# Expert results added into a table of sums by an accumulating indirect DMA, in place of rows stored and gathered at the end

## The chip, the cores and the metric

The kernel runs on one core of one Trainium2 chip, as one program with one launch. The metric is the device time of that core in microseconds (us); less is better. The engines of the core are TensorE (PE in the profile, with its weight loads as PEld), VectorE (DVE), ScalarE (ACT), GpSimd (POOL) and SyncE (SP). SP, ACT and POOL can issue DMA transfers, and 16 DMA engines carry them.

## The reference

The program computes two transformer blocks for 512 tokens of width 1024. The change touches only the last part of the second block, a layer of 32 routed experts followed by a layer norm. Cut to that part:

```python
logits = xt @ w_router + b_router                   # (512, 32)
top_vals, top_idx = lax.top_k(logits, 4)            # four experts for each token
gates = jax.nn.softmax(top_vals, axis=-1)
def expert_block(xb, e):
    gt = jnp.minimum(xb @ w_gate[e] + b_gate[e], 7.0)
    up = jnp.clip(xb @ w_up[e] + b_up[e], -7.0, 7.0)
    hid = gt * jax.nn.sigmoid(1.702 * gt) * (up + 1.0)
    return hid @ w_down[e] + b_down[e]
# for each token: the sum over its four experts of gate * expert_block(token, expert)
out = zeros.at[row_tok].add(y_rows * row_gate[:, None])
x = layer_norm_2(DEEPNORM_ALPHA_2 * h + out, ln2_g, ln2_b)
```

All numbers are float32. The matrices of one expert (gate, up and down) are 1024 x 1024 each, so 12 MB for one expert.

## The kernel before

The program is a list of stages, written by hand: every engine has its own instruction list in each stage, and semaphores join them. Nothing is scheduled by a planner. Between two stages all engines meet, and SP clears the semaphores of the stage that ended. Six earlier stages compute the first block and the attention of the second. One of them, `stage_ffn`, has no part in the experts, but its ACT list begins with transfers that write zeros to device memory. Then come the three stages that matter here.

`stage_route` scores the experts, picks four for each token, and packs the 2048 choices into **slots** of 64 rows (`CAP`), each slot with one expert. The number of slots is known only on the chip (`G.last_slot`); with these inputs there are 45. A loop over 16 columns of choices (`TK`) ends the stage: DVE makes a one-hot of the row in the slot (`colhot`) and a one-hot of the slot times twice the token number (`slothot`), and PE multiplies the two and accumulates. DVE turns the sum into `G.slot_tokens`, the list of rows to gather for each slot. It also computes `G.choice_row`, the place of each choice in the table of results.

`stage_experts` makes one **pass** per slot. A slot's 64 rows are held on 128 partitions, as two halves of 512 columns. In pass i, PE does the first half of the gate product of slot i, then transposes the hidden values of slot i-1 (`turn_h`) and the gathered rows of slot i+1 (`turn_x`), then the second half of gate(i), then down(i-1), then up(i). SP streams the matrices of the next expert into `expert_ring` (4 MB for each of the three matrices, in four parts) as soon as the last pass of the present expert has used a part. POOL gathers the rows of slot i+1 by an indirect DMA into `slot_x`; there is one such buffer, so the gather waits for the transpose of the slot before. DVE evicts down(i-1) from PSUM into `slot_y` (`result`), and ACT stores it with two plain transfers to `expert_rows` (`store`). There is one `slot_y` too: the next `result` waits for the stores.

`stage_final` reads the results back. POOL gathers 16 times 128 rows of 4 KB (four tiles of 128 tokens, four choices each) into eight buffers `choice_y`; DVE scales each by its gate and adds it into `ffn_sum`, adds ALPHA times `X`, and does the moments and the normalizing of the layer norm (class `Norm`); ACT takes the root; POOL multiplies by the gain and adds the shift (`gain_shift`); SP stores the tile.

Of the kernel before, what the change touches and what calls it, by code (L numbers as in the profile page):

```python
# [7 lines left out]
F32 = mybir.dt.float32  # L8
# [7 lines left out]
P = 128  # L16
# [1076 lines left out]
def stage_ffn(nc, A, G):  # L1093


    with ExitStack() as ctx:
# [15 lines left out]
        @block.sync  # L1112
        def _(sp):
            ln.load(sp)
            G.W.upto(sp, G.W.index[("q2",)] + RING)
            sp.wait_ge(G.y_zeroed, 16 * (-(-(MAX_SLOTS - EXPERTS) * CAP // P)))
# [427 lines left out]
def stage_route(nc, A, G):  # L1544
# [6 lines left out]
    with ExitStack() as ctx:  # L1551
# [20 lines left out]
        tok2 = sb("token_twice", [P, T])  # L1572
        upper = sb("upper_half", [P, 1])
# [12 lines left out]
        rowf = sb("choice_rowf", [P, TK])  # L1586
        colhot = sb("col_onehot", [P, 2, P])
        slothot = sb("slot_token", [P, 2, LIST])
        cmp_ = sb("slot_compare", [P, LIST, E])
        sef = sb("slot_expertf", [P, LIST])  # L1590
        names = "in lg_done iota_ok step exp_ok mem_ok cnt_done hot_ok hot_used list_done neg_ok".split()
# [9 lines left out]

        @block.gpsimd
# [12 lines left out]
        def _(pe):  # L1615
# [23 lines left out]
        def _(dve):  # L1639
# [4 lines left out]
            nc.vector.tensor_scalar(tok2[:], tok[:], 2.0, None, ALU.mult)  # L1644
# [3 lines left out]
            nc.vector.tensor_scalar(upper[:], tok[:, 0:1], float(CAP), None, ALU.is_ge)  # L1648
# [55 lines left out]
            step(nc.vector.tensor_reduce(sl[:], pick[:], AX_X, ALU.add))  # L1704
            step(nc.vector.tensor_tensor(sl[:], sl[:], over[:], ALU.add))
            for c in range(TK):
                if c >= 2:
                    dve.wait_ge(q["hot_used"], c - 1)
                nc.vector.tensor_scalar(colhot[:, c % 2, :], rank[:], col[:, c:c + 1], None, ALU.is_equal)
                nc.vector.tensor_scalar(slothot[:, c % 2, :], iota[:, 0:LIST], sl[:, c:c + 1],  # L1710
                                        tok2[:, c // TOP_K:c // TOP_K + 1], ALU.is_equal, ALU.mult).then_inc(q["hot_ok"], 1)
# [4 lines left out]
            step(nc.vector.tensor_scalar(G.slot_tokens[:], ps[:, 3, 0:LIST], upper[:, 0:1], None, ALU.add))  # L1716
# [33 lines left out]
def stage_experts(nc, A, G):  # L1750
# [5 lines left out]
    with ExitStack() as ctx:  # L1756
        def sb(name, shape, dt=F32):
# [7 lines left out]
        ids = sb("slot_ids", [P, 1], I32)  # L1765
        gt = sb("gate_act", [P, HALF])
# [7 lines left out]
                 "y_ok").split()  # L1774
# [36 lines left out]
        def _(pool):  # L1811
# [21 lines left out]
            pool.wait_ge(q["x_turned"], 1)  # L1833
            gather(1)
            last = loop(pool, body)

            pool.wait_ge(G.xg_in, last * 16 + 32)

            pool.wait_ge(G.y_out, last * 32 + 32)

        @block.scalar
        def _(act):
# [18 lines left out]
            def store(i):  # L1861
                act.wait_ge(q["y_ok"], i + 1)
                for h in range(2):
                    act.dma_start(G.y_dram[bass.ds(i * CAP, CAP), h * HALF:(h + 1) * HALF],
                                  y[h * CAP:(h + 1) * CAP, :]).then_inc(G.y_out, 16)

            def body(i, first):
# [5 lines left out]
                if not (isinstance(i, int) and i == 0):  # L1873
                    store(i - 1)
# [288 lines left out]
```

## Time and profile before

| | |
|---|---|
| Device time, median of 3 runs | 2791.09 us (2789.03 to 2792.38) |
| The profiled execution's own time | 2787.3 us |
| Its span in the profile | 2785.6 us |
| Granted TensorE clock, mean | 0.933 of full speed |
| Busy share of the span: PE, DVE, ACT, POOL | 89%, 22%, 11%, 10% |
| Bytes moved by DMA | 570.63 MB, mean 205 GB/s |
| Stage of the routing, from the span's start | 1407.2 to about 1456 us |
| Stage of the experts | about 1456 to 2723.3 us |
| Last stage | 2723.3 to 2785.6 us |

How to read it: the shares are means over stages with different limits. The profiled execution is one run; its time stands 3.8 us under the median of the three timed runs. A sum that is made against the profile is carried over to the median by the difference that it gives.

### The profile page before, as it was taken

To read this page: it belongs to the slowest core of one execution; us is meant where nothing else is said; L and a number is where in the kernel's file an instruction comes from. 1 tells how busy PE (TensorE), PEld (TensorE's weight loads), DVE (VectorE), ACT (ScalarE), POOL (GpSimd) and SP (SyncE) were. 2 spreads that over 40 slices of the span, in tenths; PEclk is the share of its full clock that TensorE was granted. 3 is DMA by queue.
4 is the path that set the end of the run, shared out by engine and by line. 5 is a ranking of instruction groups with operands and counts; after the bars stand their busy time and mean duration, and the time that the engine had idled before them with its cause. 6 is when DMAs were issued, how large, how long until landed. Compare 5 with 4: busy or idle time off the path is not lost. (4 is left out here: it accounts for less than half of the span.)

```text
span 2785.6 us, 25073 instructions
## 1 busy us (share of the span) xinstructions
PE 2474.5 (89%) x9812; PEld 1029.4 (37%) x9813; DVE 601.4 (22%) x1283; ACT 293.8 (11%) x598; POOL 277.8 (10%) x290
## 2 busy tenths in 40 slices
PE   4999999798999999895949889999999889998990
PEld 3445666343444444343443223333332223322320
DVE  1322566521000002223341101111111101110116
ACT  0111222300000000012001000100100000100000
POOL 0003111011101011111210000000000000000005
PEclk8999999899999999998959989999999989999995
DMA  7353222204312211300049998778768998879844
GB/s 290 118 202 89 76 84 91 83 0 187 126 61 91 91 60 46 137 31 0 23 195 357 419 421 312 275 264 339 302 218 339 421 418 314 333 297 421 318 179 168
DMA packets 191387, 570.63 MB, mean 205 GB/s; under 512 B 14751, under 2 KB 49692, under 8 KB 189276
## 3 DMA queue, kind: packets, MB, share of 16 engines
q1 hardware_dynamic: 172288, 526.05, 49.2%
q10 hardware_dynamic: 12764, 22.25, 2.3%
q0 software_dynamic: 6272, 21.50, 2.1%
q8 instruction: 39, 0.64, 0.1%
q14 instruction: 24, 0.20, 0.0%
HBM read 545.57 MB, written 24.18 MB: 205 GB/s over the span
## 5 line engine op out<-in xcount | busy, mean ns | idle before, releaser
L1907 PE MATMUL banks<-expert_ring,slot_xT_gate 128*64 128x512 f32 x1440 | 371.4, 663 | 67.7 <-DMA expert_ring<-in_w_gate_dram 67.0
L1907 PE MATMUL banks<-expert_ring,hiddenT 128*64 128x512 f32 x1440 | 320.6, 598 | 0.7 <-ACT hiddenT L1855 0.7
L1907 PE MATMUL banks<-expert_ring,slot_xT_up 128*64 128x512 f32 x1440 | 318.9, 595 | 0.0
L1160 PE MATMUL banks<-hT,weight_ring 128*128 128x512 f32 x512 | 223.8, 598 | 6.8 <-PEq L2080 4.6
L1178 PE MATMUL banks<-weight_ring,hidden_T 128*128 128x512 f32 x512 | 220.7, 593 | 1.5 <-PE banks L1160 1.1
L1907 PEld LDWEIGHTS banks<-expert_ring,slot_xT_gate 128*64 128x64 f32 x1440 | 108.9, 151 | 294.9 <-issue 278.5
L1907 PEld LDWEIGHTS banks<-expert_ring,hiddenT 128*64 128x64 f32 x1440 | 99.8, 137 | 217.8 <-issue 216.9
L1907 PEld LDWEIGHTS banks<-expert_ring,slot_xT_up 128*64 128x64 f32 x1440 | 99.4, 137 | 216.4 <-issue 216.4
L1160 PEld LDWEIGHTS banks<-hT,weight_ring 128*128 128x128 f32 x512 | 97.4, 192 | 132.7 <-issue 132.7
L1914 PE MATMUL banks<-bias_rows,ones 1*64 1x512 f32 x540 | 145.0, 613 | 0.0
L1178 PEld LDWEIGHTS banks<-weight_ring,hidden_T 128*128 128x128 f32 x512 | 97.0, 190 | 125.3 <-issue 125.3
L461 PE MATMUL banks<-hT,weight_ring 128*128 128x512 f32 x320 | 141.7, 603 | 0.0
L1952 DVE TENSOR_SCALAR gate_act<-banks 128x512 f32<-128x512 f32 x45 | 31.1, 692 | 469.8 <-PE banks L1914 469.8
L1820 POOL COPY slot_ids<-slot_tokens 128x1 int32 (+1 forms) x46 | 8.3, 181 | 1117.5 <-PE banks L1888 1117.4
L1050 PE MATMUL banks<-weight_ring,mixT 128*128 128x512 f32 x256 | 112.0, 600 | 5.0 <-DVE mixT L1073 5.0
L702 PE MATMUL banks<-hT,weight_ring 128*128 128x512 f32 x256 | 115.5, 606 | 0.0
L1960 DVE TENSOR_SCALAR up_act<-banks 128x512 f32<-128x512 f32 x45 | 31.1, 692 | 323.2 <-PE banks L1914 323.2
L1851 ACT COPY slot_xT_up<-banks 128x512 f32<-128x512 f32 x46 | 27.0, 586 | 651.7 <-PE banks L1914 651.7
L1972 DVE COPY slot_y<-banks 128x512 f32<-128x512 f32 x45 | 31.1, 692 | 276.8 <-PE banks L1914 276.8
L461 PEld LDWEIGHTS banks<-hT,weight_ring 128*128 128x128 f32 x320 | 61.4, 194 | 79.0 <-issue 79.0
L1050 PEld LDWEIGHTS banks<-weight_ring,mixT 128*128 128x128 f32 x256 | 49.0, 192 | 67.9 <-issue 58.7
L1203 DVE TENSOR_TENSOR ffn_out<-ffn_out,banks 128x512 f32<-128x512 f32 x24 | 16.5, 688 | 245.6 <-PE banks L1178 245.6
(349 smaller groups left out, 2067.1 us busy)
## 6 DMA issues: line engine op xcount, KB each, us to landing
expert_ring<-in_w_gate_dram SPq DMA_DIRECT2D x128, 1024.0 KB, 10.3
expert_ring<-in_w_up_dram SPq DMA_DIRECT2D x128, 1024.0 KB, 16.5
expert_ring<-in_w_down_dram SPq DMA_DIRECT2D x128, 1024.0 KB, 7.9
weight_ring<-in_w_ada_dram SPq DMA_DIRECT2D x12, 2048.0 KB, 11.4
weight_ring<-in_w_in_dram SPq DMA_DIRECT2D x8, 2048.0 KB, 13.6
weight_ring<-in_w_ff_in_dram SPq DMA_DIRECT2D x8, 2048.0 KB, 8.5
weight_ring<-in_w_ff_out_dram SPq DMA_DIRECT2D x8, 2048.0 KB, 7.9
weight_ring<-in_w_in_dram SPq DMA_DIRECT2D x24, 512.0 KB, 6.6
```

The costliest lines, as they stand in the source:

```text
L461: m = nc.tensor.matmul(ps[:, n % 4, :], w[:, k, b * P:(b + 1) * P], G.hT[:, k, :], start=(k == 0), stop=(k == KB - 1))
L702: x = nc.tensor.matmul(out, w[:, k, :], G.hT[:, k, :], start=(k == 0), stop=(k == KB - 1))
L1050: m = nc.tensor.matmul(ps[:, 2 * t + h, :], G.mixT[:, k, t * P:(t + 1) * P], w[:, k % 4, h * HALF:(h + 1) * HALF], start=(k == 0), stop=(k ...
L1160: m = nc.tensor.matmul(ps[:, n % 4, :], w[:, k, (b % 4) * P:(b % 4 + 1) * P], G.hT[:, k, :], start=(k == 0), stop=(k == KB - 1))
L1178: m = nc.tensor.matmul(ps[:, 4 + n % 4, :], aT[:, g % 2, k, t * P:(t + 1) * P], w[:, k % 4, h * HALF:(h + 1) * HALF], start=(k == 0), stop ...
L1203: nc.vector.tensor_tensor(y, y, ps[:, 4 + n % 4, :], ALU.add).then_inc(dn_read, 1)
L1851: nc.scalar.copy(flat(xTu), ps[:, B_X, :]).then_inc(q["xu_ok"], 1)
L1907: x = nc.tensor.matmul(ps[h * CAP:(h + 1) * CAP, bank, :], lhs[:, k % 4, (k // 4) * CAP:(k // 4 + 1) * CAP], X.ring[:, m, k, h * HALF:(h + ...
L1914: x = nc.tensor.matmul(ps[h * CAP:(h + 1) * CAP, bank, :], G.ones[0:1, 0:CAP], X.rows[0:1, m, h * HALF:(h + 1) * HALF], start=False, stop= ...
L1952: nc.vector.tensor_scalar(gt[:], ps[:, B_G, :], 7.0, None, ALU.min).then_inc(q["g_read"], 1)
L1960: nc.vector.tensor_scalar(up[:], ps[:, B_U, :], 7.0, -7.0, ALU.min, ALU.max).then_inc(q["u_read"], 1)
L1972: nc.vector.tensor_copy(y[:], ps[:, B_D, :]).then_inc(q["y_ok"], 1)
```

## The change

The results of the experts are no longer stored as rows and gathered at the end. A table `expert_sums` with one row for each token (1024 half rows, and 128 more as a place for the padding of the slots) is set to zero in `stage_ffn`. In the route stage POOL makes a second one-hot, of the slot times the gate, and the same matrix product then gives both the rows and the gates of every slot (`G.slot_gates`). In each pass DVE scales the evicted result by the slot's gates, and POOL adds the 128 half rows to the table by an indirect DMA with an addition. Each such addition is issued after the one before has landed. The last stage loads four tiles of sums with plain transfers. The core of the diff:

```diff
 # stage_ffn, ACT
-            for r in range(EXPERTS * CAP, MAX_SLOTS * CAP, P):
-                n = min(P, MAX_SLOTS * CAP - r)
-                act.dma_start(G.y_dram[r:r + n, :], zeros[0:n, :]).then_inc(G.y_zeroed, 16)
+            for t in range(T):
+                act.dma_start(sums[t * P:(t + 1) * P, :], zeros[:]).then_inc(G.y_zeroed, 16)
+            for table in (G.sum_dram, G.h_dram):
+                act.dma_start(table.rearrange("(r h) n -> r (h n)", h=2)[S:S + CAP, :], zeros[0:CAP, :])\
+                   .then_inc(G.y_zeroed, 16)
...
 # stage_route, POOL
+            pool.wait_ge(q["sl_ok"], 1)
+            for c in range(TK):
+                if c >= 2:
+                    pool.wait_ge(q["hot_used"], c - 1)
+                nc.gpsimd.tensor_scalar(slothot[:, c % 2, LIST:], iota[:, 0:LIST], over[:, c:c + 1],
+                                        gates[:, c:c + 1], ALU.is_equal, ALU.mult).then_inc(q["gate_hot_ok"], 1)
 # stage_route, PE
                 pe.wait_ge(q["hot_ok"], c + 1)
-                nc.tensor.matmul(ps[:, 3, 0:LIST], colhot[:, c % 2, :], slothot[:, c % 2, :], start=(c == 0),
+                pe.wait_ge(q["gate_hot_ok"], c + 1)
+                nc.tensor.matmul(ps[:, 3, 0:2 * LIST], colhot[:, c % 2, :], slothot[:, c % 2, :], start=(c == 0),
                                  stop=(c == TK - 1)).then_inc(q["hot_used"], 1)
 # stage_route, DVE
+            nc.vector.scalar_tensor_tensor(out=val[:].rearrange("p (t k) -> p t k", k=TOP_K),
...
+            nc.vector.tensor_copy(over[:], sl[:]).then_inc(q["sl_ok"], 1)
...
-            step(nc.vector.scalar_tensor_tensor(out=rowf[:], in0=sl[:], scalar=float(CAP), in1=col[:], op0=ALU.mult,
-                                                op1=ALU.add))
-            nc.vector.tensor_copy(G.choice_row[:], rowf[:])
             dve.wait_ge(q["hot_used"], TK)
+            nc.vector.tensor_copy(G.slot_gates[:], ps[:, 3, LIST:2 * LIST])
...
 # stage_experts, POOL
-            def body(i, first):
-                pool.wait_ge(q["x_turned"], i + 1)
-                gather(i + 1)
+            def scatter(i):
+                if not (isinstance(i, int) and i == 0):
+                    pool.wait_ge(G.y_out, i * 16)
+                    pool.wait_ge(q["y_ok"], i)
+                at = slice(i, i + 1) if isinstance(i, int) else bass.ds(i, 1)
+                nc.gpsimd.tensor_copy(share[:], G.slot_gates[:, at]).then_inc(q["share_ok"], 1)
+                nc.gpsimd.tensor_copy(out_ids[:], G.slot_tokens[:, at]).then_inc(q["out_ids_ok"], 1)
+                pool.wait_ge(q["out_ids_ok"], i + 1)
+                pool.wait_ge(q["y_ok"], i + 1)
+                nc.gpsimd.tensor_tensor(tick[:, 2:3], tick[:, 0:1], tick[:, 0:1], ALU.add).then_inc(q["result_held"], 1)
+                nc.gpsimd.indirect_dma_start(G.sum_dram[:, :], bass.IndirectOffsetOnAxis(out_ids[:, 0:1], 0), y[:], None,
+                                             compute_op=ALU.add).then_inc(G.y_out, 16)
...
+            with pool.Fori(2, last + 1) as i:
+                pool.wait_ge(q["x_turned"], i + 1)
+                gather(i + 1)
+                scatter(i - 1)
+            scatter(last)
 # stage_experts, ACT: store() and its two act.dma_start are gone
 # stage_experts, DVE
+                dve.wait_ge(q["share_ok"], i + 1)
                 if not first:
-                    dve.wait_ge(G.y_out, i * 32)
-                nc.vector.tensor_copy(y[:], ps[:, B_D, :]).then_inc(q["y_ok"], 1)
+                    dve.wait_ge(G.y_out, i * 16)
+                nc.vector.tensor_scalar(y[:], ps[:, B_D, :], share[:, 0:1], None, ALU.mult).then_inc(q["y_ok"], 1)
 # stage_final
+            for t in range(T):
+                sp.dma_start(sums[:, t, :], rows[t * P:(t + 1) * P, :]).then_inc(sum_in[t], 16)
...
-            for c in range(TK):
-                if c >= 8:
-                    pool.wait_ge(added, c - 7)
-                nc.gpsimd.indirect_dma_start(yk[:, c % 8, :], None, G.y_dram[:, :],
-                                             bass.IndirectOffsetOnAxis(G.choice_row[:, c:c + 1], 0))\
-                    .then_inc(in_[c % 8], 16)
...
+            ln.load(act)
...
+            for t in range(T):
+                dve.wait_ge(sum_in[t], 16)
+                nc.vector.scalar_tensor_tensor(out=G.X[:, t, :], in0=G.X[:, t, :], scalar=ALPHA, in1=sums[:, t, :],
+                                               op0=ALU.mult, op1=ALU.add).then_inc(ln.u_ok, 1)
+                ln.moments(dve, t)
+                ln.norm(dve, t)
```

The first place is the loop of POOL over the passes. Before, one turn of it is these rows (`slot_ids` is the list of rows for the gather, `tick` a dummy that keeps two instructions in order):

```order
L1820 COPY slot_ids<-slot_tokens 128x1
L1821 REGISTER_ALU
L1815 TENSOR_TENSOR tick<-tick 1x1
L1823 DMA slot_x<-h_halves,slot_ids 128x512
L1789 ISA
L1789 COMPARE_AND_BRANCH
```

And one turn of it in the changed kernel (`slot_gate` and `slot_out_ids` are the gates and the destination rows of the slot whose result is due):

```order
L1840 COPY slot_ids<-slot_tokens 128x1
L1841 REGISTER_ALU
L1835 TENSOR_TENSOR tick<-tick 1x1
L1843 DMA slot_x<-h_halves,slot_ids 128x512
L1848 ISA
L1851 ISA
L1851 COPY slot_gate<-slot_gates 128x1
L1852 REGISTER_ALU
L1852 COPY slot_out_ids<-slot_tokens 128x1
L1855 TENSOR_TENSOR tick<-tick 1x1
L1856 DMA expert_sums<-slot_y,slot_out_ids 1152x512
L1869 ISA
```

The gather now has a second indirect DMA behind it on the same engine, and the gather of the next turn stands behind that one's waits.

The second place is DVE in the last stage, one tile of four. Before:

```order
L2035 TENSOR_SCALAR ffn_sum<-choice_y,choice_gates 128x1024
L2032 SCALAR_TENSOR_TENSOR ffn_sum<-choice_y,choice_gates,ffn_sum 128x1024 x3
L2038 SCALAR_TENSOR_TENSOR X<-X,ffn_sum 128x1024
L961 BN_STATS ln2b_stats<-X 128x6
L962 BN_STATS ln2b_stats<-X 128x6
```

In the changed kernel, where `ffn_sum` holds the loaded sums:

```order
L2052 SCALAR_TENSOR_TENSOR X<-X,ffn_sum 128x1024
L961 BN_STATS ln2b_stats<-X 128x6
L962 BN_STATS ln2b_stats<-X 128x6
L963 BN_AGGR ln2b_mv<-ln2b_stats 128x2
L964 TENSOR_SCALAR ln2b_mv<-ln2b_mv 128x1
```

Four instructions of each tile are gone, and those of the layer norm follow one another directly.

## Rows read from the trace of the kernel before

**Rows 1.** Windows of the experts' stage: us, five engines' busy time, PE clock, DMA share, GB/s

```profile
1528.00:1685.90 157.90, 136.84 (x582) 43.18 (x580) 17.30 (x25) 11.92 (x20) 6.75 (x15) 0.90 1.03 420
1690.00:1860.00 170.00, 170.00 (x786) 53.84 (x784) 23.54 (x34) 16.70 (x28) 9.45 (x21) 1.00 0.74 274
```

**Rows 2.** Waits of PE from 1456 us on: total, times, longest

```profile
PE banks L1907 <- DMA expert_ring<-in_w_gate_dram: 67.0, 19, 4.9
```

**Rows 3.** Windows of the last stage, columns as in rows 1

```profile
2723.30:2735.70 12.40, 0.00 (x0) 0.00 (x0) 4.61 (x5) 1.28 (x1) 8.99 (x10) 0.50 0.91 338
2735.70:2777.70 42.00, 0.00 (x0) 0.00 (x0) 39.30 (x40) 0.81 (x4) 24.67 (x13) 0.50 0.43 162
2777.70:2785.60 7.90, 0.00 (x0) 0.00 (x0) 0.00 (x0) 0.00 (x0) 4.67 (x2) 0.50 0.17 66
```

**Rows 4.** Timeline of the last stage, DVE on the second and third tile

```profile
2744.82 1.23 DVE L2038 SCALAR_TENSOR_TENSOR X<-X,ffn_sum 128x1024 f32<-128x1024 f32 x1
2748.27 1.52 DVE L974 TENSOR_SCALAR X<-X,ln2b_mv 128x1024 f32<-128x1024 f32 x1
2752.64 3.17 DVE L2032 SCALAR_TENSOR_TENSOR ffn_sum<-choice_y,choice_gates,ffn_sum 128x1024 f32<-128x1024 f32 x1
```

**Rows 5.** The same on POOL, third tile

```profile
2764.85 2.78 POOL L982 TENSOR_TENSOR X<-X,ln2b_gb 128x1024 f32<-128x1024 f32 x1 [6.84 <-DVE X L974]
2767.71 3.20 POOL L984 TENSOR_TENSOR X<-X,ln2b_gb 128x1024 f32<-128x1024 f32 x1
```

**Rows 6.** Chain that ended last: start us, us, what; first tile's first and last

```profile
2735.70 1.23 DVE X L2038
...
2739.14 0.81 DVE X L974
```

**Rows 7.** DMA issues of the page: count, KB each, median us to landing

```profile
X<-in_x_dram SPq DMA_DIRECT2D x4, 512.0 KB, 5.6
out_dram<-X SPq DMA_DIRECT2D x4, 512.0 KB, 2.6
```

**Rows 8.** DMA queues of the page: packets, MB, share of 16 engines

```profile
q1 hardware_dynamic: 172288, 526.05, 49.2%
q10 hardware_dynamic: 12764, 22.25, 2.3%
```

**Rows 9.** Landing times of all gathers of slot_x, then of all stores

```profile
DMA to landing us min/median/max: 3.2/5.9/6.6
DMA to landing us min/median/max: 2.3/5.6/7.9
```

**Rows 10.** Timeline, one gather of POOL, and the last passes

```profile
2655.04 0.18 POOL L1820 COPY slot_ids<-slot_tokens 128x1 int32 x1 [28.96 <-PE banks L1888]
2655.86 0.99 POOL L1823 DMA_INDIRECT slot_x<-h_halves,slot_ids  x1 [0.37 <-issue]
2667.63 0.69 DVE L1972 COPY slot_y<-banks 128x512 f32<-128x512 f32 x1 [6.04 <-PE banks L1914]
2679.51 0.60 PE L1888 MATMUL banks<-ident,slot_x 128*128 128x128 f32 x4
2692.87 0.69 DVE L1972 COPY slot_y<-banks 128x512 f32<-128x512 f32 x1 [6.04 <-PE banks L1914]
2713.53 0.69 DVE L1972 COPY slot_y<-banks 128x512 f32<-128x512 f32 x1 [11.32 <-PE banks L1914]
2714.40 1.13 ACTq L1864 DMA_DIRECT2D expert_rows<-slot_y  x2
```

**Rows 11.** Groups of the route stage by shape: busy us, mean ns

```profile
L1635 PE MATMUL banks<-slot_token,col_onehot 128*128 128x64 f32 x32 | 8.9, 435 | 10.1 <-DVE slot_token L1710 10.1
```

**Rows 12.** Transposes of slot_x on PE: duration ns min/median/max

```profile
L1888 PE MATMUL banks<-ident,slot_x x184: 272/273/476, 1460.7 to 2679.8; 128*128 128x128 f32 x184
```

**Rows 13.** Timeline of the start of the ffn stage

```profile
679.18 29.90 PE L1160 MATMUL banks<-hT,weight_ring 128*128 128x512 f32 x64 [4.64 <-PEq L2080]
680.13 15.59 ACTq L1135 DMA_DIRECT2D expert_rows<-zeros  x16
```

More of the change, by code:

```diff
@@ L1600, in _ @@
             G.experts.prefetch(sp)
+        gates = G.gates[:].rearrange("p t k -> p (t k)")
         @block.gpsimd
@@ L1765, in stage_experts @@
         ids = sb("slot_ids", [P, 1], I32)
+        out_ids = sb("slot_out_ids", [P, 1], I32)
+        share = sb("slot_gate", [P, 1])
         gt = sb("gate_act", [P, HALF])
@@ L1832, in _ @@
             gather(0)
-            pool.wait_ge(q["x_turned"], 1)
-            gather(1)
-            last = loop(pool, body)
+            for i in (1, 2):
+                pool.wait_ge(q["x_turned"], i)
+                gather(i)
+            scatter(0)
+            last = pool.value_load(G.last_slot[0:1, 0:1], min_val=EXPERTS - 1, max_val=MAX_SLOTS - 1)
+            with pool.Fori(2, last + 1) as i:
[3 more added lines that the diff above has]
+            scatter(last)
             pool.wait_ge(G.xg_in, last * 16 + 32)
-            pool.wait_ge(G.y_out, last * 32 + 32)
+            pool.wait_ge(G.y_out, last * 16 + 16)
         @block.scalar
@@ L1859, in sigmoid @@
                 nc.scalar.activation(sg[:], gt[:], ACT.Sigmoid, scale=1.702).then_inc(q["sg_ok"], 1)
[L1861 to L1865, printed above, removed]
             def body(i, first):
@@ L1872, in body @@
                 sigmoid(i)
-                if not (isinstance(i, int) and i == 0):
-                    store(i - 1)
                 act.wait_ge(q["u_done"], i + 1)
@@ L1881, in _ @@
             h_turned(last)
-            store(last)
         @block.tensor
@@ L1993, in stage_final @@
         sem = G.sem
-        yk = sb("choice_y", [P, 8, D])
-        acc = sb("ffn_sum", [P, D])
-        in_ = G.choice_in
-        added, acc_step, out_done = sem("added"), sem("acc_step"), sem("out_done_all")
+        sums = sb("ffn_sum", [P, T, D])
+        sum_in = [sem(f"sum_in{t}") for t in range(T)]
+        out_done = sem("out_done_all")
         ln = Norm(nc, ctx, G, "ln2b", A["ln2_g_2"][0:1, :], A["ln2_b_2"][0:1, :])
+        rows = G.sum_dram.rearrange("(r h) n -> r (h n)", h=2)
         block = ctx.enter_context(nc.Block())
@@ L2026, in _ @@
         def _(dve):
-            for c in range(TK):
-                t, k = c // TOP_K, c % TOP_K
-                dve.wait_ge(in_[c % 8], 16 * (c // 8 + 1))
-                if k:
-                    dve.wait_ge(added, c)
-                    nc.vector.scalar_tensor_tensor(out=acc[:], in0=yk[:, c % 8, :], scalar=G.gates[:, t, k:k + 1],
-                                                   in1=acc[:], op0=ALU.mult, op1=ALU.add).then_inc(added, 1)
-                else:
-                    nc.vector.tensor_scalar(acc[:], yk[:, c % 8, :], G.gates[:, t, 0:1], None, ALU.mult).then_inc(added, 1)
-                if k == TOP_K - 1:
-                    dve.wait_ge(added, c + 1)
-                    nc.vector.scalar_tensor_tensor(out=G.X[:, t, :], in0=G.X[:, t, :], scalar=ALPHA, in1=acc[:],
-                                                   op0=ALU.mult, op1=ALU.add).then_inc(ln.u_ok, 1)
-                    ln.moments(dve, t)
-                    ln.norm(dve, t)
+            for t in range(T):
[4 more added lines that the diff above has]
+                ln.norm(dve, t)
 def make_shared(nc, ctx, A):
@@ L2064, in make_shared @@
     G.gate_bias_in, G.xg_in = sem("gate_bias_in"), sem("xg_in")
-    G.choice_in = [sem(f"choice_in{i}") for i in range(8)]
     return G
```

35 lines of the change are left out of this document (20 added, 15 removed).

## The prediction

> **What bounds the kernel now.** I read the windows of the experts' stage first, then the waits of PE, then the last stage. In the experts' stage the reader should see two kinds of passes. Where each pass brings a new expert, as in the 157.9 us from 1528.0 to 1685.9, which hold five passes (31.6 us each), the DMA engines are full: share 1.03 at 420 GB/s, and PE is busy for 136.84 us at a granted clock of 0.90 [rows 1]. Where experts have several slots, as from 1690 to 1860, PE is busy all the time at full clock and the DMA share is 0.74 [rows 1]; such a pass takes 25.24 us, the distance of two evictions of the result (2667.63 and 2692.87) [rows 10]. PE's wait for the gate matrix, 67.0 us in 19 waits [rows 2], counts the passes of the first kind: 19. So a microsecond more of DMA work per pass is paid 19 times in full and elsewhere not at all.
>
> The last stage is a chain of its own: 12.4 us until the first gathered rows are added, 42.0 us in which DVE is busy for 39.30 us, and 7.9 us of POOL and the last store, 62.3 us together [rows 3].
>
> **The last stage, removed and left.** The 16 gathers and 16 weighted additions go. What is left: four loads of 512 KB, then for each tile DVE's addition of ALPHA times X and the layer norm. The first tile lands after about 4.0 us: a lone 512 KB store takes 2.6 us and four loads in a row have a median of 5.6 us [rows 7]; the gain and the shift now come from another queue at the same time, so I take a value between them. The first tile's DVE work, uncovered by POOL, is 4.25 us, from the addition at 2735.70 to the end of the normalizing at 2739.14 + 0.81 [rows 6]. For tiles two to four, DVE's addition now starts exactly when POOL starts the gain of the tile before. An addition of this form beside POOL took 3.17 us, against 1.23 us without it [rows 4]; so 4.25 + 1.94 = 6.2 us per tile. POOL needs 2.78 + 3.20 = 6.0 us per tile beside DVE [rows 5], just under that. If the normalizing is slowed too (1.52 us once, against 0.81) [rows 4, 6], it is 6.9 us. The tail of 7.9 us stays [rows 3]. Sum: 4.0 + 4.25 + 3 x 6.2 + 7.9 = 34.75 us, in place of 62.3: **-27.5 us**. Bounds: 32 us (tile one at 3, nothing slowed twice) to 38 us (5.6 and 6.9), so -30 to -24.
>
> **The pass: DMA work.** The stores leave ACT's queue, and 256 KB per pass go by an accumulating DMA. A copy of 0.262 MB costs, at the rate of ACT's queue (22.25 MB in 2.3% of 2785.6 us on all 16 engines), 0.75 us of all 16 engines [rows 8]; at the rate of the weights' queue (526.05 MB in 49.2%) it is 0.68 us [rows 8]. The trace shows no accumulating transfer. It must bring in two streams, the result and the old sum, and write one. Lower bound of its extra price: 0, if the read of the old sum hides in the pipeline of reads and writes. Likeliest: the input side carries twice the bytes, so it costs one copy more, 0.7 us. Upper bound: each row waits for memory before the next goes. Nearly all of the shortest store's 2.3 us [rows 9] is fixed time, and each engine has 8 of the 128 rows, so up to 8 x 2.3 - 0.7 = 18 us per pass. That end is far, but nothing in the trace excludes it. I take 0.7, since an engine that is full at 1.03 with three kinds of transfers in flight shows that the queues overlap well [rows 1]: 19 x 0.7 = **+13.3 us**. The Trainium skill (DMA: Bandwidth & Descriptors, "SDMA does more than copy") calls the addition an inline unit that reduces two streams and gives no price for it; no run here has shown it yet. By the reading that inline means free, this term would be 0 and the total 13.3 us lower.
>
> **The pass: the order on POOL.** Before, the gather of slot i+2 left as soon as slot i+1 was transposed, a pass ahead. Now it stands behind the addition of result i-1, which waits for DVE's eviction. Take the pass at 2667.63 [rows 10]: the result is out at 2668.3, the dummy and the issue of the addition take about 0.5 + 1.0 us, the turn of the loop about 0.3, then copy of the list to start of the gather 2655.86 - 2655.04 = 0.8 us. The gather starts at about 2671. Landing takes 3.2 to 6.6 us [rows 9], so 2674.3 to 2677.7; the rows are wanted by the transpose at 2679.5. The slack is 1.8 us at worst. The addition's traffic is ahead of the gather on the same queue, which I price at up to a copy or two, 0.7 to 1.4 us. So it fits, barely, and costs 0. In the long passes there are 6 us more. Where the cover is gone, each lost microsecond stands on PE's path in up to 24 short passes. The other waits are long over: the gates of slot i are copied a pass ahead of `result`, and the addition before has landed some 15 us before the next eviction. DVE's scaled eviction is of the same form and shape as the copy. ACT loses two issues and waits for nothing else. For the last pass, the store issued at 2714.40 with its 1.13 us for two issues landed at about 2715.05 + 2.3 = 2717.3 [rows 9, 10]. The addition starts at about 2715.0 and lands after the shortest gather, 3.2 us [rows 9], plus an estimated 1.2 for the second read: 2719.4. **+2.1 us**, bounds 0.5 and 6.
>
> **The route stage.** The matrix product of each choice goes from 64 to 128 columns. At the same low clock one PE instruction takes 435 ns for 64 columns [rows 11] and 476 for 128 [rows 12]; two per choice, and one choice in two lies on the ring of DVE and PE, so 8 x 2 x 0.04 = 0.7 us. DVE adds two small operations and a copy on its path, 0.4 us by their size, and drops two that lay beside PE. POOL's one-hot has no row; from 2.78 us for 1024 columns of two inputs [rows 5], 64 columns are 0.17 us plus a start of about 0.2 (its copy of one column takes 0.18 [rows 10]); it runs beside DVE's two operations. Bounds 0 and 0.3 us for each of 8 rounds. Sum **+1.5 us**, 0.5 to 4. Five more semaphores to clear: 0.2 us.
>
> **The zeros.** Ten of 16 transfers go from the start of the ffn stage, where ACT spends 15.59 us issuing them [rows 13]. PE works through its 64 products from 679.18 on for 29.90 us in one piece [rows 13], which covers ACT's issues: 0. Without that cover the fewer issues would be a gain of some 9 us.
>
> **Sum.** Against the profiled execution's own 2787.3 us: -27.5 + 13.3 + 2.1 + 1.5 + 0.2 = -10.4, so 2776.9. That execution stands 3.8 us under the median, so in the medians it is 2791.1 - 10.4 = **2780.7 us**.
>
> **Rivals.**
> - *The second stream is free.* The price per pass is under 0.3 us; total -24 to -18 us, 2767 to 2773. For it: writes and reads are separate sides of a transfer. Against it: the DMA share of 1.03 leaves no gap for more reads [rows 1]. Chance 0.22.
> - *The accumulating transfer is slow* (the other side of zero). Place: the 19 full passes. It decides from 23.7 / 19 = 1.25 us more per pass on, where the gain is used up. At four times a copy, 2.1 us more, it costs 40 us, total +16: 2807. At the far end, 18 us per pass, it is +300 us. For it: additions in the transfer path work on elements, and nothing shows their rate. Chance 0.25, of which a fifth above 2820.
> - *The gather comes late.* Place: the transpose of `slot_x` in the short passes. It decides when the addition holds the queue for over 1.8 us. Each microsecond late in the half of 24 short passes with loads in flight is 12 us, so 2 us late gives -10.4 + 24 = +14: 2804. Against it: the shortest landing leaves 5 us. The Trainium skill (DMA: Bandwidth & Descriptors, "Two DMAs through the same engine are not ordered") says that only the completion semaphore orders transfers, and the diff waits for one per pass; by it the wait stands on POOL alone, as worked out above. Chance 0.08.
> - *The last stage gives little*, because the loads or DVE beside POOL take longer: -15 instead of -27.5, total +2: 2793. Chance 0.05.
> - My forecast, -17 to -3 us, 2774 to 2788: chance 0.40.
>
> **Numbers.** The measurement tells 0.2% (5.6 us) from no change. Faster by more: all of the first rival, most of the forecast (down to 0.9 us per pass) and a little else, 0.56. Within 0.2%: 0.17. Slower: 0.27. The range of eight in ten is 2765 to 2815; the forecast's own is 2774 to 2788.
>
> **What would show it.** The last stage 33 to 37 us long, with DVE's addition of tiles two to four near 3.2 us. The full passes near 32.3 us in place of 31.6, the short ones still 25.24, with no wait of PE for `slot_x`. Landing of the additions 4 to 9 us. The route stage 1 to 2 us longer. I am wrong if the full passes grow by over 1.3 us, or if short passes are longer than 25.3 us.

## The result and the profile after

The changed kernel takes 2800.0 us, the median of 10 runs (2797.61 to 2801.23), against 2791.09 us for the kernel before (10 runs, 2787.16 to 2795.17). The ratio is 1.0031 with an interval of 1.0021 to 1.0040: **slower by 0.3%**, 8.9 us, where 10.4 us less were forecast. The two profiled spans stand 12.7 us apart, 2785.6 and 2798.3 us. The granted clock is no cause: its mean is 0.933 before and 0.934 after.

A **full pass** is here one of the 19 in which PE waits for the gate matrix [rows 2], a short one any other. First the windows, the view of [rows 1] and [rows 3]: the same five full passes near the stage's start, then the last stage in three stretches. The columns are the busy times of PE, PEld, DVE, ACT and POOL with their counts, the clock, the DMA share and GB/s.

```profile
1534.99:1699.30 164.31, 136.89 (x582) 43.34 (x580) 17.59 (x25) 11.93 (x20) 17.54 (x35) 0.91 1.03 401
2760.85:2767.24 6.39, 0.00 (x0) 0.00 (x0) 0.00 (x1) 1.28 (x1) 0.00 (x0) 0.50 0.81 250
2767.24:2790.41 23.17, 0.00 (x0) 0.00 (x0) 21.52 (x28) 0.81 (x4) 16.70 (x6) 0.50 0.28 112
2790.41:2798.30 7.89, 0.00 (x0) 0.00 (x0) 0.00 (x0) 0.00 (x0) 4.68 (x2) 0.50 0.33 133
```

Five full passes take 164.31 us in place of 157.9. PE's busy time is the same to 0.1 us (136.89 and 136.84 us), and the DMA share is at 1.03 as before, but it carries 401 GB/s where it carried 420 [rows 1]. So the DMA engines are as full as they were and move less. The last stage takes 6.39 + 23.17 + 7.89 = 37.45 us in place of 62.3 [rows 3].

The waits of PE from 1450 us on (total, times, longest), in the view of [rows 2]:

```profile
PE banks L1934 <- DMA expert_ring<-in_w_gate_dram: 96.5, 19, 6.3
PE banks L1915 <- DMA slot_x<-h_halves,slot_ids: 6.6, 1, 6.6
PE banks L1648 <- POOL slot_token L1616: 2.1, 5, 0.4
```

The 19 waits for the gate matrix grew from 67.0 to 96.5 us, by 29.5. The wait for `slot_x` is the one of the very first pass, before which nothing has been loaded. The third row is in the route stage: PE waits there for POOL's one-hot, which didn't exist before.

The queues of the page, as [rows 8] (packets, MB, share of 16 engines), then two of its DMA issues (count, median us from issue to landing):

```profile
q1 hardware_dynamic: 172576, 527.10, 49.7%
q0 software_dynamic: 10448, 24.91, 3.6%
q10 hardware_dynamic: 4348, 5.99, 0.6%
...
expert_sums<-slot_y,slot_out_ids POOLq DMA_INDIRECT x45, 7.8
...
slot_x<-h_halves,slot_ids POOLq DMA_INDIRECT x46, 6.7
```

The median gather lands 0.8 us later than before (6.7 against 5.9 us [rows 9]).

Adding the pieces up from the distance between evictions of the result: the first result comes at 1503.30 us instead of 1497.94 (+5.4); the 19 full passes last 617.9 us together instead of 589.2 (+28.8, 32.52 us each instead of 31.01); the other 25 take 626.4 us in both (24 short ones at 25.24 us each and the last distance at 20.66); from the last result to the last stage it is 2760.85 - 2747.65 = 13.2 us instead of 9.8 (+3.4); the last stage gives back 24.9. Sum +12.7 us, the whole of the difference of the spans.

### The profile page after: what moved, and what is told of

Same layout as the page of the kernel before. It is cut to its first block and busy times, and to the rows that moved or that the text cites. A ratio compares the mean times of both kernels' runs of the same rounds, so it can differ in the third digit from the quotient of the medians.

```text
span 2798.3 us, 25242 instructions
## 1 busy us (share of the span) xinstructions
PE 2476.7 (89%) x9812; PEld 1031.2 (37%) x9813; DVE 581.3 (21%) x1270; ACT 294.0 (11%) x598; POOL 373.4 (13%) x470
## 5 line engine op out<-in xcount | busy, mean ns | idle before, releaser
L1934 PE MATMUL banks<-expert_ring,slot_xT_gate 128*64 128x512 f32 x1440 | 371.9, 664 | 97.2 <-DMA expert_ring<-in_w_gate_dram 96.5
L1855 POOL TENSOR_TENSOR tick<-tick 1x1 f32<-1x1 f32 x45 | 8.3, 184 | 879.6 <-DVE slot_y L2000 879.6
L2000 DVE TENSOR_SCALAR slot_y<-banks,slot_gate 128x512 f32<-128x512 f32 x45 | 33.8, 751 | 277.0 <-PE banks L1941 277.0
L1856 POOL DMA_INDIRECT expert_sums<-slot_y,slot_out_ids x45 | 72.6, 1612 | 23.3 <-issue 23.3
```

What stands on the lines that cost most here:

```text
L1856: nc.gpsimd.indirect_dma_start(G.sum_dram[:, :], bass.IndirectOffsetOnAxis(out_ids[:, 0:1], 0), y[:], None, compute_op=ALU.add).then_inc(G ...
L1934: x = nc.tensor.matmul(ps[h * CAP:(h + 1) * CAP, bank, :], lhs[:, k % 4, (k // 4) * CAP:(k // 4 + 1) * CAP], X.ring[:, m, k, h * HALF:(h + ...
L2000: nc.vector.tensor_scalar(y[:], ps[:, B_D, :], share[:, 0:1], None, ALU.mult).then_inc(q["y_ok"], 1)
```

## The theories

The growth of the full passes is over twice what the addition was priced at (13.3 us), so it was this that the experiments had to explain. Three theories, each able to hold beside the others:

- **The ring's place** (theory A in the expectations). In SBUF `expert_ring` stands behind the small tiles of the stage before. The change puts `G.slot_gates` (256 bytes of each partition) where `G.choice_row` (64 bytes) was, and so moves the ring by 192 bytes: worked out from the kernel's allocations, it began at byte 37888 = 148 x 256 of each partition, and now begins at 38080, which is no multiple of 256. If the weights' packets (the pieces of 4 KB in which a transfer is recorded) are slower for it, every full pass pays.
- **The addition itself**: the transfer that reads, adds and writes costs more of the DMA engines than a copy. This was the prediction's term. The expectations add a variant, their theory B: the additions also slow the weights' packets beside them.
- **The order on POOL** (theory C): the gather behind the addition needn't be late for its reader to cost something. It now falls into the stretch in which the next gate matrix is loaded, and PE waits for that matrix.

## The experiments

Nine kernels; each ratio is to the kernel before on the same chip. The runs fell on several chips, on which the kernel before has medians from 2788.6 to 2791.09 us, so differences between two of the kernels are taken from their ratios or from their profiles. Times of full passes are sums over the 19, from evictions in one profile. How far such a sum can be trusted is seen where two kernels have the same passes: 600.07 and 600.09 us (the two shifts of the ring), 611.7 and 611.4 (the two pads), 604.95 and 604.81 (the two with an early gather and the addition). PE's wait for the gate matrix alone is rougher: it is 83.2 and 79.9 us in the two shifts of the ring, whose passes sum to the same 600.1; where PE computes longer it waits less.

### The ring shifted in the kernel before

Only an unused tile ahead of the ring is added, so that the ring begins where it does after the change.

```diff
         G.last_slot = sbc(ctx, "last_slot", [P, 1], I32)
+        G.spare = sbc(ctx, "spare", [P, 48])
```

> The kernel before with one unused tile of 192 bytes per partition ahead of the expert ring, so that the ring begins where it begins in the changed kernel (byte 38080 of each partition, 192 above a multiple of 256) and not at 37888 (148 times 256). Nothing else is changed. Theory A (the place of the ring makes each weight packet slower): full passes grow by about 0.7 to 0.9 us of 31.6, 19 of them, so 13 to 17 us slower, and weight packets no longer all take 0.159 us. Theory B (the accumulating transfers slow the weight transfers beside them): no change, within 3 us.

2797.68 us, ratio 1.0031 (1.0020 to 1.0041). An unused tile costs as much as the whole change does, though less than the 13 to 17 us expected. The full passes take 600.1 us (+10.9), and PE's wait for the gate matrix is 83.2 us. The window over the same five passes as [rows 1], PE's waits, and the queues as in [rows 8]:

```profile
1525.54:1687.04 161.50, 136.51 (x582) 43.04 (x580) 17.31 (x26) 11.94 (x20) 6.75 (x15) 0.90 1.03 410
```

```profile
PE banks L1907 <- DMA expert_ring<-in_w_gate_dram: 83.2, 19, 6.0
```

```profile
q1 hardware_dynamic: 172288, 526.05, 49.6%
q10 hardware_dynamic: 12764, 22.25, 2.4%
```

The same work at the same share, now at 410 GB/s. The packets and bytes of the weights' queue are the same as before, to the last digit, and they take 49.6% of 2793.9 us instead of 49.2% of 2785.6 [rows 8]: 1385.8 against 1370.5, 15 us more of all 16 engines (the shares are rounded to 0.1%, 2.8 us). The loads that pass PE by in the short passes carry some of that unseen.

The DMA records show it packet by packet. Of the 95325 weight packets of 4 KB in the experts' stage, nearly all take 0.159 us when the ring is in its old place: 2.8% take over 0.160 us. With the shift it is 44.7%, and the mean goes from 0.1648 to 0.1676 us. The pad moves the tiles behind the ring too, `slot_x` among them, but these packets are the ring's own.

### The same with 128 bytes

```diff
+        G.spare = sbc(ctx, "spare", [P, 32])
```

> The kernel before with an unused tile of 128 bytes per partition ahead of the ring, which then begins at byte 38016, 128 above a multiple of 256. If any offset from a multiple of 256 makes the packets slower: as with 192 bytes, 8 us slower, about 2797. If only offsets that are no multiple of 128 count: no change, 2789.

2797.83 us, ratio 1.0031 (1.0021 to 1.0040), full passes 600.1 us; 36.1% of the weight packets take over 0.160 us. The window over the same five passes:

```profile
1528.43:1689.53 161.10, 137.19 (x582) 43.27 (x580) 17.30 (x26) 11.95 (x20) 6.79 (x15) 0.90 1.03 410
```

An offset of 128 bytes from a multiple of 256 costs what one of 192 does. The Trainium skill (DMA: Bandwidth & Descriptors, "How a descriptor splits into AXI transactions") states that a transaction begins at a multiple of 256 bytes, so a descriptor that starts off one fetches bytes that it doesn't use; it states this of what is read. By it and its beats of 32 bytes, a packet of 4096 bytes, 128 beats, would need 4 more at an offset of 128, an estimated 3%, and 6 more at 192, an estimated 5%. Here the side that is off is SBUF's, the one that is written, so no run tests the statement as it stands. What is measured is 161.1 us for the five passes at 128 and 161.5 at 192, against 157.9 in the old place: 2.0% and 2.3%. So the cost is of that order at 128, but that 192 costs half as much again is not seen. Why the offset costs anything stays open.

### The ring put back in the changed kernel

Two kernels, with pads that bring the ring to 38912 = 152 x 256 and to 38144 = 149 x 256.

```diff
         G.last_slot = sbc(ctx, "last_slot", [P, 1], I32)
+        G.spare = sbc(ctx, "spare", [P, 208])
```

> The changed kernel with one unused tile of 832 bytes per partition ahead of the expert ring, which begins at byte 38912 (38 times 1024; before it was at 37 times 1024). Theory A: full passes shrink from 33.1 to about 32.3 us, which is the 0.7 us of my prediction over 31.6; total 13 to 17 us less than the changed kernel's 2800, so 2783 to 2787, and faster than the kernel before by 4 to 8 us. Theory B: 2800 as it was.

```diff
+        G.spare = sbc(ctx, "spare", [P, 16])
```

> The same with an unused tile of 64 bytes, so that the ring begins at 38144 (149 times 256, but no multiple of 512). Theory A with a multiple of 256 as what counts: as the run with 832 bytes, 2783 to 2787. Theory A with a multiple of 512 or 1024: somewhere between that and 2800. Theory B: 2800.

2791.81 us (1.0007, 0.9998 to 1.0016) and 2791.98 us (1.0004, 0.9995 to 1.0013). Both undo most of the loss, so it is not the size of the pad but where the ring begins. They give back less than the 13 to 17 us expected. The full passes fall from 617.9 to 611.7 and 611.4 us, and the share of weight packets over 0.160 us falls from 47.0% to 6.3% and 6.5%. The first one's wait:

```profile
PE banks L1934 <- DMA expert_ring<-in_w_gate_dram: 91.3, 19, 5.7
```

So the ring's place is worth 0.24 to 0.31%, some 7 to 8.6 us. With that out of the way, the change as it was meant is within the measurement of the kernel before, and still not a gain. Of the full passes' +28.8 us, 22.5 remain.

### The addition left out

The rows are written into the table instead of added, so the sum over a token's experts is left out: the last of the four writes stands. The ring is off the multiple as in the changed kernel.

```diff
-                nc.gpsimd.indirect_dma_start(G.sum_dram[:, :], bass.IndirectOffsetOnAxis(out_ids[:, 0:1], 0), y[:], None,
-                                             compute_op=ALU.add).then_inc(G.y_out, 16)
+                nc.gpsimd.indirect_dma_start(G.sum_dram[:, :], bass.IndirectOffsetOnAxis(out_ids[:, 0:1], 0), y[:], None)\
+                    .then_inc(G.y_out, 16)
```

> The changed kernel, its ring where it was, with the indirect transfer of the results as a plain write in place of an addition (the output then holds the last expert's rows and not the sum: the sum over the experts is left out). Theory that the addition costs one copy more per pass: 19 x 0.74 = 14 us less, 2786, and the engine time of these packets falls from 0.176 to 0.084 us for 2 KB. Theory that the addition also slows the weights: 28 us less, 2772.

2789.7 us, 1.0003 (0.9994 to 1.0011); against the changed kernel's 1.0031 that is 0.28% less, 8 us. The full passes take 608.3 us, 9.6 less. The indirect queue carries the same bytes:

```profile
q0 software_dynamic: 7568, 24.91, 2.3%
```

Of 3.6% of the span it needs 2.3% now, 36 us of engine time for 45 additions, 0.8 us each. That is the one copy more that the prediction took (0.7 us). In the DMA records a 2 KB packet of the addition has a median of 0.176 us. A 2 KB packet of ACT's plain stores in the kernel before has 0.084, and the plain indirect write goes in half as many packets, of 4 KB and 0.159 us. Theory B is not borne out: the mean weight packet takes 0.1679 us beside the additions and 0.1685 beside the plain writes.

### The gather ahead of the addition

Ring at 38912. POOL issues the gather of slot i+2 before it waits for the result of slot i-1, as in the kernel before; the last slot but one gets its addition behind the loop, with an index of its own that DVE computes.

```diff
+            pool.wait_ge(q["x_turned"], 3)
+            gather(3)
             scatter(0)
...
-            with pool.Fori(2, last + 1) as i:
-                pool.wait_ge(q["x_turned"], i + 1)
-                gather(i + 1)
+            with pool.Fori(2, last) as i:
+                pool.wait_ge(q["x_turned"], i + 2)
+                gather(i + 2)
                 scatter(i - 1)
+            scatter(pool.value_load(G.last_slot[0:1, 1:2], min_val=EXPERTS - 2, max_val=MAX_SLOTS - 2))
             scatter(last)
```

> The changed kernel with its ring on a multiple of 1024 bytes and POOL's order altered: the gather of the next slot leaves as soon as its buffer is free, before the wait for the result, as in the kernel before, and the addition follows it. Theory C (the gather, now behind the addition, falls into the stretch in which PE's next gate matrix is being loaded, and so delays it): PE's wait for the gate matrix falls from 91.3 to about 80 us, the full passes by some 8 us in all, and the total from 2791.8 to about 2783, 0.2% faster than the kernel before. Rival (what is left over the addition's own engine time comes from the indirect transfer by POOL's queue in place of ACT's two plain stores): no change, 2791 to 2792.

2786.65 us, 0.9981 (0.9972 to 0.9990). Against the ratio of the padded kernel, 1.0007, that is 0.26% less, 7 us, and the full passes fall by as much: 604.95 us in place of 611.7.

```profile
PE banks L1938 <- DMA expert_ring<-in_w_gate_dram: 85.6, 19, 5.6
```

### The gather late in the kernel before

The other way round: the kernel before with nothing but its gather held back until the result of the slot before is out.

```diff
                 pool.wait_ge(q["x_turned"], i + 1)
+                if not first:
+                    pool.wait_ge(q["y_ok"], i - 1)
                 gather(i + 1)
```

> The kernel before with one wait more on POOL: each gather waits for DVE's eviction of the result, as it does in the changed kernel, with the stores still plain and on ACT. Theory C: full passes grow by 6 to 9 us in all, total 2795 to 2798. Rival: the place of the gather costs nothing, 2789.

2794.86 us, 1.0015 (1.0006 to 1.0024), 4 to 5 us more than the kernel before on that chip (median 2789.64). Full passes 596.5 us (+7.3), the ring in its old place. PE waits for the gate matrix and not for `slot_x`:

```profile
PE banks L1909 <- DMA expert_ring<-in_w_gate_dram: 75.5, 19, 4.9
```

So the order costs 4 to 7 us in either kernel, without any reader of the gather waiting for it behind the first pass. One full pass shows where the gather went; the kernel before, then this one (POOL's gather, SP's first issues of the next gate matrix):

```profile
1611.78 0.99 POOL L1823 DMA_INDIRECT slot_x<-h_halves,slot_ids  x1 [0.38 <-issue]
1624.89 1.53 SPq L1737 DMA_DIRECT2D expert_ring<-in_w_gate_dram  x3
```

```profile
1624.17 0.99 POOL L1823 DMA_INDIRECT slot_x<-h_halves,slot_ids  x1 [0.37 <-issue]
1623.84 1.55 SPq L1737 DMA_DIRECT2D expert_ring<-in_w_gate_dram  x3
```

The DMA records say the same of all 19. Between SP's first issue of the gate matrix and the end of PE's wait for it, the kernel before has no packet of a gather; with the gather late, all of a gather's packets lie there, 0.26 MB that take 0.65 us of the 16 engines. That stretch grows from 10.06 to 10.51 us on average.

### Early gather and plain write together

The kernel with the early gather, with the addition left out as above (what is left out is again the sum over a token's experts).

```diff
 # the kernel with the early gather, POOL
-                nc.gpsimd.indirect_dma_start(G.sum_dram[:, :], bass.IndirectOffsetOnAxis(out_ids[:, 0:1], 0), y[:], None,
-                                             compute_op=ALU.add).then_inc(G.y_out, 16)
+                nc.gpsimd.indirect_dma_start(G.sum_dram[:, :], bass.IndirectOffsetOnAxis(out_ids[:, 0:1], 0), y[:], None)\
+                    .then_inc(G.y_out, 16)
```

> As e5 (ring on a multiple of 1024 bytes, early gather), with the indirect transfer of the results as a plain write in place of an addition (the sum over the experts is left out). If an addition costs the DMA engines one copy more and nothing else: 0.74 us in each of 19 full passes, 14 us less than e5's 2786.7, about 2773; if the full passes hide a part of it, as between the changed kernel (2800.0) and its plain form (2789.7), 10 us less, 2777. PE's wait for the gate matrix falls to the 67 us of the kernel before or a little above.

2775.95 us, 0.9957 (0.9945 to 0.9968), 0.24% or 7 us under the kernel with the addition (0.9981); full passes 594.3 us, 10.6 less.

```profile
PE banks L1938 <- DMA expert_ring<-in_w_gate_dram: 70.4, 19, 4.7
```

So the addition costs 0.5 to 0.56 us per full pass (9.6 and 10.6 us over 19), with the ring off its place and on it. It leaves 594.3 - 589.2 = 5.2 us that no theory named: the results go through POOL's indirect queue instead of ACT's plain stores. That it is this is only what is left over.

### Which full passes pay

Seven of the 19 full passes follow a short one or are the first; twelve follow a full one. In the kernel before the DMA engines are full all through the twelve (share 1.02 to 1.03), while in the short pass ahead of six of the seven their share is 0.71 to 0.73. The sums of the two groups, as differences from profile to profile in us:

| What differs | The seven | The twelve |
|---|---|---|
| Ring off by 192, by 128, in the kernel before | -0.3, +0.8 | +11.2, +10.2 |
| Ring off by 192, changed kernel against the pad of 832 bytes | +1.5 | +4.7 |
| Gather late, in the kernel before | +4.9 | +2.4 |
| Gather late against early, changed kernel with the ring in place | +4.6 | +2.2 |
| Addition against plain write, ring in place and gather early | +1.3 | +9.3 |
| Addition against plain write, changed kernel | +2.9 | +6.7 |
| What is left: early gather and plain write against the kernel before | +4.7 | +0.5 |

Two kernels with the same passes differ by up to 2.0 us in a group, so only the large entries speak. The ring and the addition cost mainly in the twelve, where every microsecond of engine time is paid: 0.6 to 0.8 us for each addition, near its 0.8 us of engine time. The late gather costs mainly in the seven, 0.65 to 0.7 us each, and that is the 0.65 us that its packets take: it leaves a short pass, in which the engines had time over, for the stretch that PE waits on. In the twelve it costs engine time wherever it stands, and moving it adds only 0.2 us each. The open 5.2 us lie in the seven too, so a dearer transfer that costs alike in every full pass is not their cause.

### The route and the last stage mended too

Ring and early gather as above; DVE makes the gate one-hot in the route stage instead of POOL (its copy of the slot numbers and PE's wait for POOL go with it), and the gain and the shift of the layer norm come behind the first tile of sums, on SP's queue.

```diff
 # stage_route, POOL: its loop of tensor_scalar is gone; DVE
+                nc.vector.tensor_scalar(slothot[:, c % 2, LIST:], iota[:, 0:LIST], sl[:, c:c + 1], gates[:, c:c + 1],
+                                        ALU.is_equal, ALU.mult)
...
 # stage_final, SP
                 sp.dma_start(sums[:, t, :], rows[t * P:(t + 1) * P, :]).then_inc(sum_in[t], 16)
+                if t == 0:
+                    ln.load(sp)
 # stage_final, ACT
-            ln.load(act)
```

> As e5, and two more edits: the one-hot of the gates is made on DVE in place of POOL, and in the last stage the gain and shift are loaded by SP behind the first tile of sums in place of ACT beside them. Theory that POOL's one-hots of 0.65 us set the pace of the route stage: the rounds of two choices take about 1.4 in place of 1.75 us, 2.5 to 3 us less. Theory that the first tile of sums lands late (6.4 us) because six transfers share the engines: it lands at about 4 us, 2 us less. In all 4 to 5 us under e5, about 2778 to 2779. Rival for the route stage: DVE's third operation for each choice is no quicker than POOL's, no gain.

2781.7 us, 0.9961 (0.9948 to 0.9975), 5 us under the early gather alone (4 to 5 expected) and 0.4% under the kernel before: the best kernel here that computes the whole sum. Two consecutive rounds of the loop over choices, two choices each, in the changed kernel and then in this one:

```profile
1446.46 1.33 PE L1648 MATMUL banks<-slot_token,col_onehot 128*128 128x128 f32 x4 [0.43 <-POOL slot_token L1616]
1448.20 1.33 PE L1648 MATMUL banks<-slot_token,col_onehot 128*128 128x128 f32 x4 [0.41 <-POOL slot_token L1616]
```

```profile
1444.60 1.44 PE L1641 MATMUL banks<-slot_token,col_onehot 128*128 128x128 f32 x4 [0.18 <-DVE slot_token L1725]
1446.22 1.44 PE L1641 MATMUL banks<-slot_token,col_onehot 128*128 128x128 f32 x4 [0.18 <-DVE slot_token L1725]
```

A round goes from 1.74 to 1.62 us, 8 x 0.12 = 1 us. In the last stage the first tile lands sooner, but the second then isn't there in time:

```profile
2745.45 0.34 SPq L2029 DMA_DIRECT2D ffn_sum<-expert_sums  x1
...
2749.00 1.22 DVE L2051 SCALAR_TENSOR_TENSOR X<-X,ffn_sum 128x1024 f32<-128x1024 f32 x1 [15.94 <-DMA ffn_sum<-expert_sums]
...
2753.42 2.33 POOL L982 TENSOR_TENSOR X<-X,ln2b_gb 128x1024 f32<-128x1024 f32 x1 [17.99 <-DVE X L974]
2753.93 2.90 DVE L2051 SCALAR_TENSOR_TENSOR X<-X,ffn_sum 128x1024 f32<-128x1024 f32 x1 [0.67 <-DMA ffn_sum<-expert_sums]
```

It takes 3.55 us to the first tile in place of 6.39, and then DVE is idle for 0.67 us before the second, whose addition now lies beside POOL and takes 2.90 us. From the last result to the end it is 48.1 us instead of 50.5. These two, 1.0 and 2.4 us, are what of the 5 us has a place. The edit moves the gain and the shift, and with them the loads of the other three tiles by 0.9 us, so which of the two makes the first tile quicker is not separated.

## Why the prediction was wrong, step by step

**The last stage: right, 2.6 us too good.** Forecast -27.5, measured -24.9 us. The tail of 7.9 us stayed (7.89), and a tile comes every 6.3 us (6.2 forecast). The first tile took 6.39 us and not 4.0, over the upper end of 5.6; the last stage of 37.45 us is still inside the bounds of 32 to 38, whose lower end doesn't come out of its own terms (3 + 4.25 + 3 x 6.0 + 7.9 is 33.2). The cadence was right by luck, for another reason than the one given. The timeline of DVE and POOL on the second tile:

```profile
2771.42 1.22 DVE L2052 SCALAR_TENSOR_TENSOR X<-X,ffn_sum 128x1024 f32<-128x1024 f32 x1
2771.66 3.18 POOL L982 TENSOR_TENSOR X<-X,ln2b_gb 128x1024 f32<-128x1024 f32 x1 [20.85 <-DVE X L974]
...
2774.86 2.94 DVE L974 TENSOR_SCALAR X<-X,ln2b_mv 128x1024 f32<-128x1024 f32 x1
2774.91 2.34 POOL L984 TENSOR_TENSOR X<-X,ln2b_gb 128x1024 f32<-128x1024 f32 x1
```

DVE's addition starts before POOL does and keeps its 1.22 us; POOL's gain pays (3.18). The normalizing then meets POOL's shift, started 0.05 us after it, and takes 2.94 us instead of 0.81. The forecast had +1.94 on the addition; it is +2.13 on the normalizing. In both pairs DVE's instruction starts first by the record, by 0.24 us where POOL's pays and by 0.05 us where DVE's pays. The kernel with the last stage mended has a pair in which POOL leads, by 0.51 us (2753.42 and 2753.93), and DVE's addition pays with 2.90 us. In these pairs the one with a clear lead keeps its time, and a lead of 0.05 us is not enough.

**The pass: DMA work: the addition right, the weights forgotten.** "It costs one copy more, 0.7 us" was confirmed in engine time (0.8 us). In all it cost 9.6 to 10.6 us in the full passes, 7 to 8 by the ratios, for 13.3 forecast. "Paid 19 times in full" was too many: near its full price it is paid in the twelve passes in which the engines are full all through. The failed step is the one that wasn't taken: this term priced what the diff does to the stores and put the 12 MB of weights of each full pass at nothing. The moved ring costs 7 to 8.6 us by the ratios, most of the 8.9 that the kernel lost. Neither the change's description nor the prediction asks what stands behind `G.choice_row` and `G.slot_gates` in memory.

**The pass: "so it fits, barely, and costs 0": the reader right, the price wrong.** This is the second failed step. The gather starts 3.8 us after the eviction (3.4 forecast), and its reader doesn't wait:

```profile
2701.75 0.75 DVE L2000 TENSOR_SCALAR slot_y<-banks,slot_gate 128x512 f32<-128x512 f32 x1 [6.04 <-PE banks L1941]
...
2703.33 1.61 POOL L1856 DMA_INDIRECT expert_sums<-slot_y,slot_out_ids  x1 [0.50 <-issue]
...
2705.56 1.02 POOL L1843 DMA_INDIRECT slot_x<-h_halves,slot_ids  x1 [0.15 <-issue]
```

```profile
2713.63 0.60 PE L1915 MATMUL banks<-ident,slot_x 128*128 128x128 f32 x4
```

But the gather's packets now lie in the stretch in which the next gate matrix is loaded, and push it back. The step looked for a late `slot_x` and not for a later gate matrix, which was the wait of 67.0 us in [rows 2]; it costs 4 to 7 us.

**The last landing: +2.3 forecast (2.1, and 0.2 for the semaphores), +3.4 measured.** No run separates the semaphores. POOL's issue of the addition takes 1.60 us where that of a gather takes 0.99, and no addition landed in under 5.0 us (3.2 plus 1.2 was the estimate):

```profile
2747.65 0.75 DVE L2000 TENSOR_SCALAR slot_y<-banks,slot_gate 128x512 f32<-128x512 f32 x1 [11.32 <-PE banks L1941]
...
2749.21 1.60 POOL L1856 DMA_INDIRECT expert_sums<-slot_y,slot_out_ids  x1 [0.48 <-issue]
2760.85 2.05 SPq L2031 DMA_DIRECT2D ffn_sum<-expert_sums  x4
```

```profile
DMA to landing us min/median/max: 5.0/7.8/9.4
```

**The route stage: +1.5 forecast, +4.3 measured.** It goes from 1406.92 to 1460.19 us, against 1407.20 to 1456.14. POOL's one-hot was estimated at 0.37 us and takes 0.65:

```profile
L1616 POOL TENSOR_SCALAR slot_token<-iota,over,choice_gates 128x64 f32<-128x64 f32 x16 | 10.3, 651 | 39.8 <-DVE over L1725 36.7 <-PE banks L1648 3.1
```

The rounds of two choices in the kernel before, from PE's timeline:

```profile
1445.58 1.12 PE L1635 MATMUL banks<-slot_token,col_onehot 128*128 128x64 f32 x4 [0.18 <-DVE slot_token L1710]
1446.88 1.12 PE L1635 MATMUL banks<-slot_token,col_onehot 128*128 128x64 f32 x4 [0.18 <-DVE slot_token L1710]
```

PE waited 0.18 us for DVE there, and now waits 0.41 to 0.43 us for POOL; the round grows from 1.30 to 1.74 us: 8 x 0.44 = 3.5 us. The first result is 1.3 us later still; in kernels with an unchanged route stage its time varies by up to 2.4 us, so nothing is read from that.

**The zeros and the short passes: right.** The short passes take 25.24 us in every kernel, and the route stage, which follows what the zeros could have delayed, starts at 1406.92 us against 1407.20.

**The rivals, and the signs.** A slow addition, a late `slot_x`, a last stage that gives little and an addition for free all did not come; the loss came from two costs that none of them had. The prediction's own sign of being wrong did come: the full passes grew by 1.5 us each, over the 1.3 that it allowed. Term by term the forecast missed by 2.6 (last stage), 15.5 (full passes), 1.1 (last landing) and 3.9 us (route stage and up to the first result), 23.1 in all and every one to the same side, so nothing cancelled. In the full passes the +28.8 us are, from profile to profile: ring 6.2 (617.9 to 611.7), order 6.8 (to 604.95), addition 10.6 (to 594.3), open 5.2 (to 589.2).

## What to carry to other kernels

When a change adds or drops a small tile that stands ahead of a large buffer filled by DMA, work out where the buffer begins before and after, and keep it on a multiple of 256 bytes of each partition; a pad of 64 bytes was worth 0.27% here. When a transfer moves in time, look whether it leaves a stretch in which the DMA engines have time over for one in which a matrix is awaited, and price it there by its engine time, not only by its own reader. And before judging an idea, take the accidents of its layout out: the addition by DMA as written lost 0.3%, and with the ring in place, the gather early, the one-hot on DVE and the gain and shift behind the first tile it gained 0.4%.

## What the runs showed of the hardware that was not expected

- The start of a DMA destination in SBUF matters: with the ring 192 or 128 bytes off a multiple of 256, 44.7% and 36.1% of its 4 KB packets took over 0.160 us, against 2.8%, and the full passes took 1.9% longer (589.2 to 600.1 us). Other offsets were not run.
- An indirect DMA with an addition costs twice a copy in the engines (a packet of 2 KB takes 0.176 us, against 0.084 in a plain store) and 1.60 against 0.99 us of POOL's issue.
- A gather of 0.26 MB costs its 0.65 us of engine time where it is moved from a stretch at a share of 0.71 to 0.73 into the one that PE waits on, and 0.2 us where the engines were full before and after.
- POOL's `tensor_scalar` with two scalars from a tile takes 0.65 us for 64 columns, against 0.31 us on DVE for the like with the same shape.
- The normalizing, a `tensor_scalar` of 1024 columns, takes 0.81 us alone and 2.94 us beside POOL; before, the same overlap was short and showed 1.52 us [rows 4].
